# More PSUM banks for the scatter, slots and gather of a two-layer decoder step's expert loop, and the scatter's add ahead of the next low part

## The chip, the cores and the metric

The kernel runs on one NeuronCore of a Trainium2 chip. The metric is the device time of one execution in microseconds (us): the median of three runs.

## The reference

One inference step of a two-layer decoder trunk for 256 prompt tokens and 64 sample tokens, 320 in all, in float32. Each layer is a mixer (window attention, a short convolution, attention into a memory), a layer norm, a feed-forward part and another layer norm. The feed-forward part is a dense SwiGLU in layer 0; in layer 1, which takes half of the time, each token goes to two of eight SwiGLU experts:

```python
def _swiglu(x, wg, wu, wd):
    return (jax.nn.silu(x @ wg) * (x @ wu)) @ wd

def _moe(x, w_router, b_router, wg, wu, wd):
    ...
    top_v, top_i = lax.top_k(logits, TOP_K)          # 2 of 8
    top_w = jax.nn.softmax(top_v, axis=-1)
    gates = jnp.sum(jax.nn.one_hot(top_i, N_EXPERTS) * top_w[..., None], axis=1)
    for e in range(N_EXPERTS):
        y = y + gates[:, e:e + 1] * _swiglu(xt, wg[e], wu[e], wd[e])
```

The width is 1024, the hidden width 2816.

## The kernel before

**Precision.** A float32 product is made from three fast ones. Each weight is split into a high part (a rounded copy) and a low part (weight minus high part), each activation likewise, and TensorE (PE) adds high x high, low x high and high x low in PSUM.

**Units.** Weights stream from HBM in units of 1 MB (128 x 2048 numbers). SyncE (SP) issues the load of a unit into a ring of 11 buffers as soon as the unit that held the buffer is done. ScalarE (ACT) writes the high part into one of three buffers (`hi_moe`, L771), so it waits for the load and for the unit three back. VectorE (DVE) writes the low part over the raw weights (`lo_moe`, L1050) when the high part is there. Both work two units ahead of PE: in iteration m they make the parts of unit m+2, and ACT can begin when unit m-1 is done.

**The expert loop.** Every engine runs a hardware loop of its own over pairs of experts (`Fori`, `step`); with these inputs it has 4 steps. Experts take at most 128 tokens at a time, in 128 slots each. A pair is 66 units, 33 an expert (n = 0 to 32; j = 0 or 1 is the expert). The hidden width is cut into halves h = 0 to 5 of 512 (the last of 256). Gate units fill PSUM bank 2 + h % 2, up units bank 4 + h % 2, and the down units (first at n = 8) add into banks 0 and 1. A unit is twelve matmuls of 512 columns (L1910 to L1912 or L1894 to L1896), and its last matmul raises `unit_done`. ACT makes silu of the gate half (L1004), DVE multiplies it by the up half (L1423), PE turns the result into bank 6 (L1919, after the units in `TURN_AFTER`), and ACT and DVE split it (`hidden_hi`, `hidden_lo`, L1403).

**Around a pair's units.** Beside the units each step does this, all of it through PSUM bank 7 before the change:

- *Scatter* (j = 0, after units 0 to 5): PE multiplies the previous pair's outputs `ygh`, `ygl` by the slot matrices, four matmuls (L1864, L1865) for one of six parts g of 128 tokens by 512 columns; DVE adds the part to the sum (`add_back`, L1410).
- *Slots* (after units 6 and 7) and *gates* (after 8): PE transposes the one-hot matrices of this pair (L1849) and sums the gates (L1856); DVE copies (L1433) or reduces them.
- *Gather* (j = 1, after units 28 to 31): ten matmuls of 256 columns (L1841 to L1843) collect two of the eight blocks of the next pair's tokens; ACT and DVE split them (`gathered`, L966, and `tokens_lo`, L1370).

Since one bank serves them all, each of these waits on PE until DVE has emptied the bank of the one before it:

```python
pe.wait_ge(scat_cp, step * 6 + g)          # scatter g: add g-1 is done
pe.wait_ge(xe_lo, step * 4 + (c + 4))      # gather c: low part c-1 is done
```

Each engine works through its own list in order. In iteration n of the loop DVE had this order: multiply (n in `MULT_AT`), low part of unit m+2, hidden low part, then the add, copy or reduction that belongs to unit n-1.

**Tables.** ACT needs a function table for Silu. The program's table loads are put in when it is compiled; in the trace each step has one ahead of its first high part (L771) and one ahead of its first silu (L1004).

Of the kernel before, what the change touches and what calls it, by code (L numbers as in the profile page):

```python
# [23 lines left out]
F32 = mybir.dt.float32  # L24
# [4 lines left out]
ALU = mybir.AluOpType  # L29
ACT = mybir.ActivationFunctionType  # L30
# [9 lines left out]
T = NP + NS  # L40
# [17 lines left out]
AHEAD = HI_RING - 1  # L58
# [75 lines left out]
TURN_AFTER = {5: 0, 9: 1, 15: 2, 21: 3, 27: 4, 29: 5}  # L134
GATHER_AFTER = {28: 0, 29: 1, 30: 2, 31: 3}
SCATTER_AFTER = {n: n for n in range(6)}
SLOTS_AFTER = {6: 0, 7: 1}
GATES_AFTER = 8
ONE_HOT_AT = 14
for (_k, _h), _n in LAST_UNIT.items():  # L140
    assert all(n > _n for n, hs in (SILU_AT.items() if _k == "g" else [(n, x) for n, xs in MULT_AT.items() for x in xs]) if hs == _h)
# [78 lines left out]
def build_trunk(nc, A, O):  # L220
    with ExitStack() as ctx:
# [33 lines left out]
        ident = take("ident", [P, P])  # L255
# [499 lines left out]
        def _(act):  # L755
# [207 lines left out]
            def gathered(first, c, bank=7):  # L963

                act.wait_ge(gath_mm, first + (c + 1))
                act.activation(xeh[:, 2 * c:2 * c + 2, :], ps[:, bank, :].rearrange("p (f s) -> p f s", s=2 * P),  # L966
                               ACT.Copy).then_inc(xe_hi, 1)
# [24 lines left out]
                residual(k)  # L992
            for c in range(1, 4):
                gathered(0, c, FIRST_BANK[c])
            act.activation(row_f[:, 3:4], eps[:, 0:1], ACT.Copy).then_inc(e_silu, 1)
            act.wait_ge(rt_total, 1)
            total = act.value_load(total_i[0:1, 0:1], min_val=PAIRS, max_val=ROUNDS * PAIRS)
            with act.Fori(0, total) as step:
                for m in range(NPAIR):
                    j, n = divmod(m, NX)  # L1000
                    hi_moe(step, m + AHEAD)
                    if n in SILU_AT:
                        h = SILU_AT[n]
                        act.activation(sil[:, h % 2, 0:HIDDEN[h][1]], ps[:, 2 + h % 2, 0:HIDDEN[h][1]],  # L1004
                                       ACT.Silu).then_inc(e_silu, 1)
                    if n - 1 in TURN_AFTER:
                        hidden_hi(step * 12 + 6 * j, TURN_AFTER[n - 1])
                    if j == 1 and n - 1 in GATHER_AFTER:
                        gathered(step * 4 + 4, GATHER_AFTER[n - 1])
                    if n == NX - 1:  # L1010
                        act.wait_ge(unit_done, step * NPAIR + (N_DENSE + m + 1))
                        act.wait_ge(slot_cp, step * 3 + 3)
                        act.activation(ygh[:, j, :], ps[:, 0:2, :].rearrange("p b n -> p (b n)"), ACT.Copy,
                                       scale=gs[:, j:j + 1]).then_inc(y_hi, 1)
# [22 lines left out]
        def _(dve):  # L1037
# [8 lines left out]
            def lo_moe(step, m):  # L1046

                s = (m + MOE_FIRST) % RING_MOE
                dve.wait_ge(hi_done, step * NPAIR + (N_DENSE + m + 1))
                dve.tensor_tensor(low_moe[s][:, :], raw_moe[s][:, :],  # L1050
                                  high[(N_DENSE + m) % HI_RING][:, :].bitcast(F32), ALU.subtract).then_inc(lo_done, 1)
# [347 lines left out]
            def hidden_lo(at, h):  # L1399
                tiles = HIDDEN[h][1] // P  # L1400
                to = slice(HID_TILE[h], HID_TILE[h] + tiles)
                dve.wait_ge(e_hi, at + (h + 1))
                dve.tensor_tensor(hel[:, to, :], ps[:, 6, 0:P * tiles].rearrange("p (f s) -> p f s", s=P),  # L1403
                                  heh[:, to, :].bitcast(F32), ALU.subtract).then_inc(e_lo, 1)

            def add_back(first, g):

                half = slice(512 * (g % 2), 512 * (g % 2) + 512)
                dve.wait_ge(scat_mm, first + (g + 1))
                dve.tensor_tensor(acc[:, g // 2, half], acc[:, g // 2, half], ps[:, 7, :], ALU.add).then_inc(scat_cp, 1)  # L1410

            dve.wait_ge(acc_cp, 6)
            dve.wait_ge(rt_total, 1)
# [1 line left out]
            with dve.Fori(0, total) as step:  # L1415
                for m in range(NPAIR):
                    j, n = divmod(m, NX)
                    at = step * 12 + 6 * j
                    for h in MULT_AT.get(n, ()):
                        width = HIDDEN[h][1]  # L1420
                        dve.wait_ge(e_silu, at + (h + 2))
                        dve.wait_ge(unit_done, step * NPAIR + (N_DENSE + NX * j + LAST_UNIT["u", h] + 1))
                        dve.tensor_tensor(sil[:, h % 2, 0:width], sil[:, h % 2, 0:width], ps[:, 4 + h % 2, 0:width],  # L1423
                                          ALU.mult).then_inc(e_h, 1)
                    lo_moe(step, m + AHEAD)
                    if n - 1 in TURN_AFTER:
                        hidden_lo(at, TURN_AFTER[n - 1])
                    if j == 0 and n - 1 in SCATTER_AFTER:
                        add_back(step * 6, SCATTER_AFTER[n - 1])
                    if j == 0 and n - 1 in SLOTS_AFTER:  # L1430
                        i = SLOTS_AFTER[n - 1]
                        dve.wait_ge(slot_mm, step * 3 + (i + 1))
                        dve.tensor_copy(slot[:, i, 0:T], ps[:, 7, 0:T]).then_inc(slot_cp, 1)  # L1433
                    if j == 0 and n - 1 == GATES_AFTER:
                        dve.wait_ge(slot_mm, step * 3 + 3)
                        dve.tensor_reduce(gs[:, :], ps[:, 7, 0:4].rearrange("p (j c) -> p j c", c=2), AX, ALU.add
                                          ).then_inc(slot_cp, 1)
                    if j == 1 and n == ONE_HOT_AT:
                        one_hot(step + 1)
                        gate_columns(step + 1)  # L1440
                    if j == 1 and n - 1 in GATHER_AFTER:
                        tokens_lo(step * 4 + 4, GATHER_AFTER[n - 1])
                    if n == NX - 1:
                        dve.wait_ge(y_hi, step * 2 + (j + 1))
                        dve.scalar_tensor_tensor(ygl[:, j, :], ps[:, 0:2, :].rearrange("p b n -> p (b n)"), gs[:, j:j + 1],
                                                 ygh[:, j, :].bitcast(F32), ALU.mult, ALU.subtract).then_inc(y_lo, 1)
# [39 lines left out]
        def _(pe):  # L1486
# [359 lines left out]
            def slots_of(j):  # L1846

                for t, (t0, tn) in enumerate(TILES):
                    last = pe.transpose(ps[:, 7, t0:t0 + tn], onehot[0:tn, t, j, :].bitcast(F32), ident[0:tn, 0:tn])  # L1849
                last.then_inc(slot_mm, 1)  # L1850

            def gates_of():
# [23 lines left out]
            with pe.Fori(0, total) as step:  # L1876
                for m in range(NPAIR):
# [36 lines left out]
                    if n in TURN_AFTER:  # L1914
                        h = TURN_AFTER[n]
                        pe.wait_ge(e_h, at + (h + 2))
                        pe.wait_ge(e_lo, at + (h + 1))
                        for f in range(HIDDEN[h][1] // P):
                            last = pe.transpose(ps[:, 6, P * f:P * f + P], sil[:, h % 2, P * f:P * f + P], ident[:, :])  # L1919
                        last.then_inc(e_tr, 1)  # L1920
                    if j == 0 and n in SCATTER_AFTER:
                        g = SCATTER_AFTER[n]
                        if g == 0:
                            pe.wait_ge(y_lo, step * 2 + 1)
                            pe.wait_ge(xe_lo, step * 4 + 4)
                        else:
                            pe.wait_ge(scat_cp, step * 6 + g)
                        scatter(ps[:, 7, :], g, 0, True, False)
                        scatter(ps[:, 7, :], g, 1, False, True).then_inc(scat_mm, 1)
                    if j == 0 and n in SLOTS_AFTER:  # L1930
                        if SLOTS_AFTER[n] == 0:
                            pe.wait_ge(scat_cp, step * 6 + 6)
                        else:
                            pe.wait_ge(slot_cp, step * 3 + 1)
                        slots_of(SLOTS_AFTER[n])
                    if j == 0 and n == GATES_AFTER:
                        pe.wait_ge(slot_cp, step * 3 + 2)
                        pe.wait_ge(gc_done, step + 1)
                        gates_of()
                    if j == 1 and n in GATHER_AFTER:  # L1940
                        c = GATHER_AFTER[n]
                        if c == 0:
                            pe.wait_ge(slot_cp, step * 3 + 3)
                            pe.wait_ge(oh_done, step + 2)
                        else:
                            pe.wait_ge(xe_lo, step * 4 + (c + 4))
                        gather(c)

            pe.wait_ge(e_h, total * 12 + 1)
            pe.wait_ge(e_lo, total * 12 + 1)  # L1950
# [39 lines left out]
```

## Time and profile before

| | us |
|---|---|
| median of 3 runs | 1709.35 (1709.29 to 1710.72) |
| the profiled execution | 1703.73 |
| its span, first to last instruction | 1702.0 |
| expert loop in it, first unit to the last unit's end | 829.3 to 1683.0 |
| the first matmuls of steps 1 to 4 | 829.29, 1044.68, 1257.88, 1472.32 |

The profile is of one execution. Engine times are busy times; a matmul's end is modelled, and matmuls overlap, so the start-to-start distance of two matmuls is their real price, and the "idle before" of PE counts only from the modelled end of the matmul before. PEld is the weight load that precedes each matmul and runs beside the one before it.

### The profile page before, as it was taken

The page shows a single profiled execution, that of the slowest core. Times are in us where ns is not written, and L with a number is a line of the kernel's source. Part 1 is how long each engine was busy: PE and PEld are TensorE (multiplying, and loading weights), DVE is VectorE, ACT ScalarE, POOL GpSimd, SP SyncE. Part 2 cuts the span into 40 slices and gives each one's busy share as a digit, 9 for nine tenths or more (in the row PEclk, how much of TensorE's full clock was granted, in tenths as well). Part 3 has the DMA queues.
Part 4 walks back from the last instruction along what each step waited for, and adds up shares of the span by engine and source line. Part 5 has one row for each costly group of instructions (what it writes and reads, how often), then busy time and mean ns, then how long its engine had stood idle before and what let it go on. Part 6 is the DMA issues. An engine that isn't in the chain of part 4 may idle for free.

```text
span 1702.0 us, 23565 instructions
## 1 busy us (share of the span) xinstructions
PE 1615.1 (95%) x9231; PEld 1413.1 (83%) x9231; DVE 1134.3 (67%) x1048; ACT 934.7 (55%) x947; POOL 62.1 (4%) x114
## 2 busy tenths in 40 slices
PE   6999999999998999998899998999989999899996
PEld 6999898999997999897678886788867888678885
DVE  4545655644435445655678887788867888778887
ACT  3544443433323644443557776577755777657775
POOL 4112000000000020001000000000000000000000
PEclk8999999999999999999999999999999999999998
DMA  9745433344443443343589997899978999789991
GB/s 292 251 127 185 122 124 124 116 151 154 150 149 100 125 153 124 104 145 136 177 283 366 364 368 249 283 365 364 368 239 278 364 365 368 254 277 365 365 325 56
DMA packets 214085, 394.63 MB, mean 232 GB/s; under 512 B 8032, under 2 KB 98544, under 8 KB 213952
## 3 DMA queue, kind: packets, MB, share of 16 engines
q1 hardware_dynamic: 208576, 379.08, 64.9%
q0 software_dynamic: 5408, 14.06, 2.7%
q8 instruction: 81, 1.33, 0.3%
q14 instruction: 20, 0.16, 0.0%
HBM read 390.32 MB, written 4.76 MB: 232 GB/s over the span
## 4 chain that ended last, share of the span: by engine, by line
PE 87%; DVE 5%; issue 4%; ACT 3%; DMA 1%; SPq 0%; DVEq 0%; ACTq 0%
PE ps L1489 12%; PE ps L1491 12%; PE ps L1490 12%; PE ps L1910 9%; PE ps L1912 9%; PE ps L1911 9%; PE ps L1894 4%; PE ps L1896 4%; PE ps L1895 4%; ACT high L771 2%; PE ps L1919 1%; PE ps L1638 1%; PE ps L1744 1%; PE ps L1738 1%; PE ps L1612 1%
## 5 line engine op out<-in xcount | busy, mean ns | idle before, releaser
L1050 DVE TENSOR_TENSOR low<-raw,high 128x2048 fp32r<-128x2048 f32 x266 | 608.6, 2291 | 154.5 <-ACT high L771 154.5
L771 ACT ACTIVATE high<-raw 128x2048 fp32r<-128x2048 f32 x266 | 509.7, 1918 | 273.7 <-PE ps L1912 168.0
L1489 PE MATMUL ps<-xh,high 128*128 128x320 f32 x1088 | 341.8, 314 | 10.3 <-DVE xl L1229 9.4
L1059 DVE TENSOR_TENSOR low<-raw,high 128x2048 fp32r<-128x2048 f32 x90 | 205.9, 2291 | 214.4 <-ACT high L764 214.2
L1490 PE MATMUL ps<-xh,low 128*128 128x320 f32 x1088 | 337.8, 310 | 0.0
L1491 PE MATMUL ps<-xl,high 128*128 128x320 f32 x1088 | 337.7, 310 | 0.0
L1910 PE MATMUL ps<-high,xeh 128*128 128x512 f32 (+1 forms) x768 | 293.5, 382 | 8.1 <-issue 7.3
L1911 PE MATMUL ps<-low,xeh 128*128 128x512 f32 (+1 forms) x768 | 289.1, 376 | 0.0
L1912 PE MATMUL ps<-high,xel 128*128 128x512 f32 (+1 forms) x768 | 288.9, 376 | 0.0
L764 ACT ACTIVATE high<-raw 128x2048 fp32r<-128x2048 f32 x90 | 171.9, 1910 | 172.7 <-PE ps L1491 156.5
L1489 PEld LDWEIGHTS ps<-xh,high 128*128 128x128 f32 x1088 | 206.2, 190 | 19.8 <-issue 19.0
L1490 PEld LDWEIGHTS ps<-xh,low 128*128 128x128 f32 x1088 | 206.4, 190 | 0.0
L1491 PEld LDWEIGHTS ps<-xl,high 128*128 128x128 f32 x1088 | 206.2, 190 | 0.0
L1910 PEld LDWEIGHTS ps<-high,xeh 128*128 128x128 f32 x768 | 144.9, 189 | 38.3 <-issue 8.6
L1912 PEld LDWEIGHTS ps<-high,xel 128*128 128x128 f32 x768 | 145.1, 189 | 29.4
L1911 PEld LDWEIGHTS ps<-low,xeh 128*128 128x128 f32 x768 | 144.9, 189 | 26.8
L1894 PE MATMUL ps<-high,heh 128*128 128x512 f32 x352 | 140.8, 400 | 0.0
L1896 PE MATMUL ps<-high,hel 128*128 128x512 f32 x352 | 139.3, 396 | 0.0
L1895 PE MATMUL ps<-low,heh 128*128 128x512 f32 x352 | 138.9, 395 | 0.0
L1896 PEld LDWEIGHTS ps<-high,hel 128*128 128x128 f32 x352 | 66.0, 187 | 16.0
L1894 PEld LDWEIGHTS ps<-high,heh 128*128 128x128 f32 x352 | 66.1, 188 | 14.7
L1895 PEld LDWEIGHTS ps<-low,heh 128*128 128x128 f32 x352 | 66.2, 188 | 14.6
(323 smaller groups left out, 1731.4 us busy)
## 6 DMA issues: line engine op xcount, KB each, us to landing
raw<-in_exp_w_gate_dram SPq DMA_DIRECT2D x90, 1024.0 KB, 5.3
raw<-in_exp_w_up_dram SPq DMA_DIRECT2D x88, 1024.0 KB, 5.3
raw<-in_exp_w_down_dram SPq DMA_DIRECT2D x88, 1024.0 KB, 5.3
raw<-in_w_in_dram SPq DMA_DIRECT2D x37, 1024.0 KB, 5.4
raw<-in_ffn_w_gate_dram SPq DMA_DIRECT2D x11, 1024.0 KB, 5.3
raw<-in_ffn_w_up_dram SPq DMA_DIRECT2D x11, 1024.0 KB, 5.3
raw<-in_ffn_w_down_dram SPq DMA_DIRECT2D x11, 1024.0 KB, 5.0
raw<-in_w_o_dram SPq DMA_DIRECT2D x8, 1024.0 KB, 5.0
```

Source lines behind the costliest of these rows:

```text
L771: act.activation(high[(N_DENSE + m) % HI_RING][:, :], raw_moe[s][:, :], ACT.Copy).then_inc(hi_done, 1)
L1050: dve.tensor_tensor(low_moe[s][:, :], raw_moe[s][:, :], high[(N_DENSE + m) % HI_RING][:, :].bitcast(F32), ALU.subtract).then_inc(lo_done, 1)
L1059: dve.tensor_tensor(low[n % RING][:, :], raw[n % RING][:, :], high[n % HI_RING][:, :].bitcast(F32), ALU.subtract).then_inc(lo_done, 1)
L1489: pe.matmul(out, wh, ah, start=first, stop=False)
L1490: pe.matmul(out, wl, ah, start=False, stop=False)
L1491: return pe.matmul(out, wh, al, start=False, stop=last)
L1894: pe.matmul(out, heh[:, tile, :], wh[:, c], start=i == 0 and k == 0, stop=False)
L1895: pe.matmul(out, heh[:, tile, :], wl[:, c], start=False, stop=False)
L1896: last = pe.matmul(out, hel[:, tile, :], wh[:, c], start=False, stop=i == NBLK - 1 and k == 1)
L1910: pe.matmul(out, xeh[:, k, slots], wh[:, c], start=k == 0, stop=False)
L1911: pe.matmul(out, xeh[:, k, slots], wl[:, c], start=False, stop=False)
L1912: last = pe.matmul(out, xel[:, k, slots], wh[:, c], start=False, stop=k == KD - 1)
```

## The change

- Scatter part g goes to bank 7, 0, 1, 7, 0, 1; its wait is now for the add three parts back, and parts 0 to 2 wait for no add. Banks 0 and 1 are free of expert outputs from the pair's end until unit 8.
- The slot matrix of expert 0 goes to bank 7, that of expert 1 to bank 6, where the hidden halves are turned: it waits for the hidden low part of half 0, and the turn after unit 9 waits for its copy. The gates wait for the first slot copy only.
- Gather c goes to bank 7, 3, 4, 7: the two in the middle wait for the last silu and for a product of halves, the fourth for the low part of the first.
- On DVE the scatter's adds, the slot copies and the gate reduction move ahead of the low part of unit m+2. The gather's low parts stay behind it.
- ACT computes a one-element Silu at the head of each step, so the Silu table is loaded there.

```diff
+SCATTER_BANK = (7, 0, 1, 7, 0, 1)
+SLOT_BANK = (7, 6)
+GATHER_BANK = (7, 3, 4, 7)
...
-            act.activation(row_f[:, 3:4], eps[:, 0:1], ACT.Copy).then_inc(e_silu, 1)
+            act.activation(row_f[:, 2:3], eps[:, 0:1], ACT.Copy).then_inc(e_silu, 1)
...
             with act.Fori(0, total) as step:
+                act.activation(row_f[:, 3:4], eps[:, 0:1], ACT.Silu)
                 for m in range(NPAIR):
...
-                        gathered(step * 4 + 4, GATHER_AFTER[n - 1])
+                        gathered(step * 4 + 4, GATHER_AFTER[n - 1], GATHER_BANK[GATHER_AFTER[n - 1]])
...
-                dve.tensor_tensor(acc[:, g // 2, half], acc[:, g // 2, half], ps[:, 7, :], ALU.add).then_inc(scat_cp, 1)
+                dve.tensor_tensor(acc[:, g // 2, half], acc[:, g // 2, half], ps[:, SCATTER_BANK[g], :],
+                                  ALU.add).then_inc(scat_cp, 1)
...
-                    lo_moe(step, m + AHEAD)
-                    if n - 1 in TURN_AFTER:
-                        hidden_lo(at, TURN_AFTER[n - 1])
                     if j == 0 and n - 1 in SCATTER_AFTER:
                         add_back(step * 6, SCATTER_AFTER[n - 1])
                     if j == 0 and n - 1 in SLOTS_AFTER:
                         i = SLOTS_AFTER[n - 1]
                         dve.wait_ge(slot_mm, step * 3 + (i + 1))
-                        dve.tensor_copy(slot[:, i, 0:T], ps[:, 7, 0:T]).then_inc(slot_cp, 1)
+                        dve.tensor_copy(slot[:, i, 0:T], ps[:, SLOT_BANK[i], 0:T]).then_inc(slot_cp, 1)
                     if j == 0 and n - 1 == GATES_AFTER:
                         dve.wait_ge(slot_mm, step * 3 + 3)
...
+                    lo_moe(step, m + AHEAD)
+                    if n - 1 in TURN_AFTER:
+                        hidden_lo(at, TURN_AFTER[n - 1])
...
-                        tokens_lo(step * 4 + 4, GATHER_AFTER[n - 1])
+                        tokens_lo(step * 4 + 4, GATHER_AFTER[n - 1], GATHER_BANK[GATHER_AFTER[n - 1]])
...
+                        if j == 0 and h == 1:
+                            pe.wait_ge(slot_cp, step * 3 + 2)
                         for f in range(HIDDEN[h][1] // P):
...
-                        else:
-                            pe.wait_ge(scat_cp, step * 6 + g)
-                        scatter(ps[:, 7, :], g, 0, True, False)
-                        scatter(ps[:, 7, :], g, 1, False, True).then_inc(scat_mm, 1)
+                        elif g >= 3:
+                            pe.wait_ge(scat_cp, step * 6 + (g - 2))
+                        scatter(ps[:, SCATTER_BANK[g], :], g, 0, True, False)
+                        scatter(ps[:, SCATTER_BANK[g], :], g, 1, False, True).then_inc(scat_mm, 1)
...
                         else:
-                            pe.wait_ge(slot_cp, step * 3 + 1)
+                            pe.wait_ge(e_lo, at + 2)
                         slots_of(SLOTS_AFTER[n])
                     if j == 0 and n == GATES_AFTER:
-                        pe.wait_ge(slot_cp, step * 3 + 2)
+                        pe.wait_ge(slot_cp, step * 3 + 1)
                         pe.wait_ge(gc_done, step + 1)
                         gates_of()
...
+                        elif c == 1:
+                            pe.wait_ge(e_silu, at + 7)
+                        elif c == 2:
+                            pe.wait_ge(e_h, at + 6)
                         else:
-                            pe.wait_ge(xe_lo, step * 4 + (c + 4))
-                        gather(c)
+                            pe.wait_ge(xe_lo, step * 4 + 5)
+                        gather(c, GATHER_BANK[c])
```

## Rows read from the trace of the kernel before

**Rows 1.** The page's first part: busy time (share of the span) and instructions.
```profile
PE 1615.1 (95%) x9231; PEld 1413.1 (83%) x9231; DVE 1134.3 (67%) x1048; ACT 934.7 (55%) x947; POOL 62.1 (4%) x114
```

**Rows 2.** Windows: length, busy by engine, granted clock, DMA share, GB/s.
```profile
1044.60:1257.80 213.20, 204.53 (x960) 165.46 (x960) 174.51 (x111) 144.40 (x100) 0.00 (x0) 1.00 0.92 326
...
1044.60:1088.00 43.40, 38.63 (x166) 29.43 (x167) 29.35 (x23) 22.81 (x16) 0.00 (x0) 1.00 0.71 239
1088.00:1159.00 71.00, 71.00 (x338) 58.31 (x337) 60.88 (x35) 52.14 (x35) 0.00 (x0) 1.00 1.00 359
```

**Rows 3.** Waits in the expert loop: total us, times, longest us.
```profile
ACT high L771 <- PE ps L1912: 168.0, 171, 3.8
...
PE ps L1864 <- DVE acc L1410: 13.3, 12, 2.1
...
PE ps L1910 <- issue: 7.3, 3, 2.6
PE ps L1841 <- DVE xel L1370: 5.3, 8, 0.7
...
PE ps L1849 <- DVE slot L1433: 3.0, 4, 0.8
...
PE ps L1856 <- DVE slot L1433: 1.7, 4, 0.5
PE ps L1849 <- DVE acc L1410: 1.4, 4, 0.5
```

**Rows 4.** Timeline around unit 3's end, step 2: start, us, instruction, idle before.
```profile
1058.61 2.29 DVE L1050 TENSOR_TENSOR low<-raw,high 128x2048 fp32r<-128x2048 f32 x1 [2.33 <-ACT high L771]
...
1059.97 0.39 PE L1912 MATMUL ps<-high,xel 128*128 128x512 f32 x1
1060.39 1.91 ACT L771 ACTIVATE high<-raw 128x2048 fp32r<-128x2048 f32 x1 [1.81 <-PE ps L1912]
...
1060.82 0.68 DVE L1410 TENSOR_TENSOR acc<-acc,ps 128x512 f32<-128x512 f32 x1
1061.42 0.68 DVE L1423 TENSOR_TENSOR sil<-sil,ps 128x512 f32<-128x512 f32 x1
...
1061.56 0.50 PE L1864 MATMUL ps<-ygh,slot 128*128 128x512 f32 x1 [1.20 <-DVE acc L1410]
...
1061.90 0.39 PE L1865 MATMUL ps<-ygl,slot 128*128 128x512 f32 x1
...
1062.13 0.40 PE L1864 MATMUL ps<-ygh,slot 128*128 128x512 f32 x1
...
1062.34 2.29 DVE L1050 TENSOR_TENSOR low<-raw,high 128x2048 fp32r<-128x2048 f32 x1 [0.23 <-ACT high L771]
```

**Rows 5.** Timeline of PE ahead of the third gather of step 1.
```profile
1032.71 0.40 PE L1896 MATMUL ps<-high,hel 128*128 128x512 f32 x1
1033.18 0.39 PE L1841 MATMUL ps<-onehot,xtokh 128*128 128x256 f32 x1
```

**Rows 6.** Timeline of PE: step 1's second scatter and after; step 3's first matmul.
```profile
838.14 0.50 PE L1864 MATMUL ps<-ygh,slot 128*128 128x512 f32 x1 [2.12 <-DVE acc L1410]
...
839.53 0.63 PE L1911 MATMUL ps<-low,xeh 128*128 128x512 f32 x1
...
842.52 0.46 PE L1912 MATMUL ps<-high,xel 128*128 128x512 f32 x1
...
1257.88 0.50 PE L1910 MATMUL ps<-high,xeh 128*128 128x512 f32 x1 [2.59 <-issue]
```

**Rows 7.** Groups in the loop: count, busy us, mean ns, idle before.
```profile
L1004 ACT ACT_TABLE_LOAD x4 | 5.1, 1283 | 0.1
...
L1433 DVE CAST slot<-ps 128x320 fp32r<-128x320 f32 x8 | 3.9, 482 | 0.0
...
L995 ACT ACTIVATE row_f<-eps 128x1 f32<-128x1 f32 x1 | 0.2, 194 | 0.0
```

**Rows 8.** SP's weight loads in step 2: time from issue to landing.
```profile
DMA to landing us min/median/max: 4.8/5.3/6.6
```

More of the change, by code:

```diff
@@ L1848, in slots_of @@
                 for t, (t0, tn) in enumerate(TILES):
-                    last = pe.transpose(ps[:, 7, t0:t0 + tn], onehot[0:tn, t, j, :].bitcast(F32), ident[0:tn, 0:tn])
+                    last = pe.transpose(ps[:, SLOT_BANK[j], t0:t0 + tn], onehot[0:tn, t, j, :].bitcast(F32), ident[0:tn, 0:tn])
                 last.then_inc(slot_mm, 1)
```

## The prediction

> **What bounds the kernel now.** I read the page first: PE is busy 95% of the span [rows 1], but its busy time is made of overlapping matmuls, so I looked at stretches of the expert loop, the only part that the diff touches. Step 2 lasts 213.2 us. The 71 us from its unit 10 on (1088 to 1159) keep PE busy all the time at a granted clock of 1.00; the first ten units, with scatter, slots and gates, leave it idle for 43.40 - 38.63 = 4.8 us [rows 2]. Then the waits. ACT waits for PE, 168.0 us behind gate and up units alone, and no wait of ACT for a load is listed. PE waits for the DVE operations that empty bank 7: 13.3 us for adds, 5.3 for gathered low parts, 3.0 + 1.4 + 1.7 around slots and gates; besides, 7.3 us of "issue" in three waits [rows 3], at the three turns of the loop. So PE is the bound, with two kinds of holes: the waits on bank 7, and the turn of the loop, which the change leaves alone.
>
> **One stall, followed.** Rows 4 show the scatter behind unit 3. The unit's last matmul starts at 1059.97 and has ended when ACT begins the next high part at 1060.39. DVE has begun a low part at 1058.61 and reaches the add of the earlier scatter, done long since, only behind it, at 1060.82. PE's scatter waits for that add and starts at 1061.56 [rows 4]. The distance from the matmul before is 1.59 us where back-to-back matmuls take 0.23 (1061.90 to 1062.13), and the following one comes after 0.34. The loss is 1.36 + 0.11 = 1.47 us, against a listed idle of 1.20: I add 0.27 to each idle of this kind, or 0.16 where the short matmuls of another operation follow.
>
> **What the change removes.**
> - Scatter: 13.3 us idle in 12 waits [rows 3], with 12 x 0.27 = 3.2: 16.5 us. Part g now waits for the add three parts back.
> - Slots and gates: 3.0 + 1.4 + 1.7 = 6.1 us in 12 waits [rows 3], with 12 x 0.16 = 1.9: 8.0 us.
> - Gather: 5.3 us in 8 waits [rows 3]; 0.16 for the four behind a unit (0.6), nothing for the four behind transposes, whose usual handover is longer. The third gather shows no idle but a distance of 0.47 for 0.23 [rows 5]: 4 x 0.24 = 1.0. Together 6.9 us.
> - One of two table loads a step: 4 x 1.28 us of ACT [rows 7]. I count nothing: in this stretch ACT idles 1.81 us before a high part, waiting for PE [rows 4]. Without that cover it would be 5.1 us.
>
> Sum: 16.5 + 8.0 + 6.9 = 31.4 us.
>
> **What it adds, and whether a stall comes back elsewhere.** A unit is 12 matmuls, 12 x 0.23 = 2.8 us, a scatter four, 0.9 us (estimates from the spacing in rows 4). Call T the end of unit m-1; times follow from T.
> - *The add ahead of the low part.* The scatter ends at about T + 1.0, the add takes 0.68 [rows 4]: done at T + 1.7. The low part can't start before ACT's high part, 1.91 us from T + 0.02 [rows 4], is done at about T + 1.95. The add fits into a gap in which DVE idles today, with 0.25 us to spare. Where a multiply comes too (unit 3 to 4), it takes 0.68 [rows 4] from T, still before the scatter ends. After unit 5 four transposes come ahead of the scatter; at four matmuls' price for them at most, the add ends at T + 2.6 and the low part is 0.7 late. That doesn't reach PE: a low part takes 2.29 [rows 4], ends at T + 4.3 on time and is read at T + 0.9 + 2.8 + 0.9 + 2.8 = T + 7.4. The margin is 3.1 us, 2.8 + 2.8 - 4.3 = 1.3 where no scatter stands between.
> - *DVE's load.* Low part, add and, once, multiply: 2.29 + 0.68 + 0.68 = 3.65 us against PE's 3.7 a unit in the scatter; elsewhere a slot copy of 0.48 [rows 7] or a hidden low part (as wide as the add, so 0.68) in place of the add: 2.8 to 3.5, for units that with slots or gates take longer than 2.8. Behind unit 7 multiply and copy stand ahead of one low part, which may then be late by some tenths; the margin there is over 1.3. So no stall on the low parts.
> - *New waits on PE.* The second slot transposes wait for the hidden low part of half 0. It stands on DVE behind the low part that ends at T + 4.3 to 5.0 (T is unit 5's end), so it is done by T + 5.7; PE gets there two units, a scatter, transposes and the first slots later, after at least 0.9 + 2.8 + 2.8 = 6.5. Behind this wait are unit 8 and all later ones, so its lateness would count in full; it has 0.8 us at least. The turn after unit 9 waits for a copy made behind unit 7, the second and third gather for a silu and a product that are two units old, the fourth for a low part three units old. Nothing.
> - *The one-element Silu* at the head of a step: 0.19 us by the like Copy [rows 7], in ACT's way to the third unit's high part. That unit's margin is the 3.1 us above. Nothing; without the cover 4 x 0.2 = 0.8.
> - *DMA.* No load moves, and SP is released by `unit_done` as before. Faster units ask for more: 66 units of 1.05 MB in 213.2 - 31.4/4 = 205.4 us, 337 GB/s, where the stretch from 1088 to 1159 gets 359 now [rows 2].
>
> **The clock.** The second scatter of step 1 starts after 2.12 us of idle. The matmuls from 839.53 to 842.52 are then 0.427 us apart, seven distances: PE is at the lower of its two levels, 1.2 GHz, instead of 2.4 [rows 6]. That costs 7 x 0.2 = 1.4 us, and as the idle goes, I take this fall to go with it. The loop's turns leave idles of up to 2.59 us [rows 6], and the change does not touch these. A fall at a turn would cost about as much, 1.4, so three turns are worth 0 to 4.2 us. The Trainium skill (TensorE: Matmul & The Clock Gate, on the clock gate's warm-up) says that the gate is either at half or at full rate and that the same kernel switches at different points from run to run. By that rule the 1.4 us might not come back, and the sum would be 31.4 instead of 32.8; no row here can decide it, as I have one execution.
>
> **The sum.** 31.4 + 1.4 = 32.8 us. Against the profiled execution, 1703.73 us, that makes 1670.9. The three timed runs have a median of 1709.35, 5.6 us above it, which I carry over: 1676.5 us.
>
> **Rivals.**
> - *Part of the stalls comes back (14 in 100).* If only the scatter gains 16.5 us, because slots and gathers find another wait (the hidden low part, or DVE's order, in which the gather's low parts stay behind the weights'), the time is 1692.9. For it: 0.25 and 0.8 us are small margins. Against it: the large ones, 1.3 to 3.1 us, stand behind them.
> - *No change, since the weights set the pace (5 in 100).* DMA's share is 1.00 from 1088 to 1159 [rows 2]. If it could do no more over a step, PE would lose at loads what it gains at banks: 1709. Against it: no wait for a load, and a load lands after 4.8 to 6.6 us in all of step 2 [rows 8], with the scatter's DMA share of 0.71 inside [rows 2], so no queue builds up.
> - *Slower: the low parts held behind the adds (3 in 100).* DVE takes its list in order, so an add whose scatter is not done holds up the low part behind it, and PE stands for that two units later. It costs PE nothing until the add ends 3.1 us after the high part, at T + 5.0. To eat 31.4 us over the four steps' 24 adds it would have to be 1.3 us later each, T + 6.3; at T + 6.8 the time would be 1709.35 - 32.8 + 24 x 1.8 = 1720. The rows give T + 1.7. The Trainium skill (PSUM — Partial Sum Buffer, Engine vs sequencer instructions) states this rule: queues of ScalarE and VectorE are strictly first in, first out. The trace agrees, since in rows 4 a finished scatter's add stands 2.2 us behind a low part; the same rule makes the old order costly and the new one risky.
>
> **How the numbers follow.** The forecast, all stalls gone, has 78 in 100 and gives 1676.5; by itself 1671 (the profiled execution's 5.6 us as a gain) to 1682 (four falls of the clock at 1.4 us more than today). The range reaches towards the partial case until it leaves out 2 in 10: 1671 to 1686. Within 0.2% (3.4 us), about what a measurement of this kernel can tell from no change, lies the case of the loads, 5 in 100; slower 3; the rest, 92, is faster.
>
> **What would show it.** Right: PE's waits for L1410's add, the slot copies and the gathered low parts vanish from the list; units 0 to 9 of step 2 take some 6 us less than 43.4; the adds stand ahead of their low parts and DVE's waits for ACT's high part shrink there; the "issue" waits remain; one table load a step. Wrong: a new wait of PE for a low part or the hidden low part in units 2 to 10, or waits of ACT for loads, or more stretches at 1.2 GHz behind the loop's turns.

## The result, and the profile after

The changed kernel takes 1665.2 us (1663.78 to 1671.1, 4 runs) against 1709.32 in four runs of the kernel before: a ratio of 0.9752 (95% interval 0.9723 to 0.9781). It is faster, as forecast, but the forecast was 1676.5 us in 1671 to 1686, so the time lies below the range. The profiled execution of the changed kernel spans 1662.1 us, 39.9 less than that of before; the sum had promised 32.8.

What I had said would vanish did vanish. The list of waits in the loop (total, times, longest us):

```profile
ACT high L774 <- PE ps L1917: 148.9, 171, 1.8
DVE low L1054 <- ACT high L774: 107.6, 198, 2.0
...
DVE acc L1414 <- PE ps L1870: 6.2, 11, 0.8
PE ps L1915 <- DVE xel L1374: 5.1, 3, 1.8
```

Against [rows 3], no wait of PE for an add, a slot copy or the next gather is left, and it is DVE that now waits for a scatter; its waits for ACT's high part fall from 151.5 us in the kernel before to 107.6. But the 7.3 us of "issue" at the turns of the loop have shrunk too, to three waits of 5.1 us in all, which the view puts down to a gathered low part. Windows of the same stretches as in [rows 2] (length, busy by engine, granted clock, DMA share, GB/s):

```profile
1032.00:1068.60 36.60, 36.56 (x163) 29.40 (x164) 29.93 (x23) 21.70 (x16) 0.00 (x0) 1.00 0.85 280
1068.60:1139.60 71.00, 71.00 (x340) 58.66 (x338) 60.69 (x35) 52.70 (x35) 0.00 (x0) 1.00 1.00 360
```

Units 0 to 9 of step 2 keep PE busy for 36.56 of 36.60 us, where they left 4.8 us idle; the stretch behind them is as it was. The timeline around unit 3's end, as in [rows 4]:

```profile
1046.06 0.39 PE L1869 MATMUL ps<-ygh,slot 128*128 128x512 f32 x1
...
1046.69 0.68 DVE L1428 TENSOR_TENSOR sil<-sil,ps 128x512 f32<-128x512 f32 x1
...
1047.29 0.68 DVE L1414 TENSOR_TENSOR acc<-acc,ps 128x512 f32<-128x512 f32 x1
1048.20 2.29 DVE L1054 TENSOR_TENSOR low<-raw,high 128x2048 fp32r<-128x2048 f32 x1 [0.24 <-ACT high L774]
```

The scatter runs on at once; multiply and add fit in ahead of the low part, which still starts when ACT's high part is done, with 0.24 us to spare.

**Where the time came from.** From the start times of the same matmuls in both timelines, all four steps together (us):

| part of the loop | before | after | less | said |
|---|---|---|---|---|
| units 0 to 9, with scatter, slots, gates | 175.3 | 146.5 | 28.8 | 24.5 + 1.4 clock |
| units 10 up to the second expert's unit 28 | 585.3 | 585.2 | 0.1 | 0 |
| the last five units, with the gather | 84.2 | 75.4 | 8.7 | 6.9 |
| three turns of the loop | 8.5 | 6.3 | 2.2 | 0 |
| the last step's end to the final scatter | 0.5 | 1.4 | -0.9 | 0 |
| loop | 853.8 | 814.8 | 39.0 | 32.8 |

In the 28.8 us are two stretches of PE at 1.2 GHz that the changed kernel does not have: the one that I had counted in step 1 (1.4 us), and a second at the start of step 3, behind the 2.59 us of idle in [rows 6]. A window there, in the kernel before, has a granted clock of 0.50:

```profile
1259.10:1262.10 3.00, 3.00 (x8) 2.32 (x7) 2.29 (x1) 0.56 (x1) 0.00 (x0) 0.50 0.28 104
```

Step 3's units 0 to 9 took 44.39 us before, step 2's 42.84: 1.55 us.

### The profile page after: what moved, and what is told of

Same layout as the page of the kernel before. It is cut to its first block, busy times and chain, and to the rows that moved or that the text cites. A ratio compares the mean times of both kernels' runs of the same rounds, so it can differ in the third digit from the quotient of the medians.

```text
span 1662.1 us, 23553 instructions
## 1 busy us (share of the span) xinstructions
PE 1603.0 (96%) x9231; PEld 1413.8 (85%) x9231; DVE 1135.4 (68%) x1048; ACT 928.8 (56%) x947; POOL 62.3 (4%) x114
## 3 DMA queue, kind: packets, MB, share of 16 engines
HBM read 390.32 MB, written 4.76 MB: 238 GB/s over the span
## 4 chain that ended last, share of the span: by engine, by line
PE 93%; DVE 3%; ACT 2%; issue 1%; DMA 1%; SPq 0%; DVEq 0%; ACTq 0%
PE ps L1494 12%; PE ps L1495 12%; PE ps L1496 12%; PE ps L1915 10%; PE ps L1917 10%; PE ps L1916 10%; PE ps L1899 5%; PE ps L1901 5%; PE ps L1900 5%; PE ps L1926 1%; PE ps L1643 1%; PE ps L1749 1%; PE ps L1869 1%; PE ps L1743 1%; PE ps L1870 1%
## 5 line engine op out<-in xcount | busy, mean ns | idle before, releaser
L1917 PEld LDWEIGHTS ps<-high,xel 128*128 128x128 f32 x768 | 144.3, 188 | 28.8
```

Of the source, the lines that this page charges most:

```text
L1917: last = pe.matmul(out, xel[:, k, slots], wh[:, c], start=False, stop=k == KD - 1)
```

## The experiments

The table has, for each kernel, the loop's parts as above (sums in us), the median length of PE's taken loop branch, and in how many steps a stretch at 1.2 GHz lies in units 0 to 9 ("falls"; one profiled execution each).

| kernel | units 0-9 | gather | turns | end | branch | falls | loop |
|---|---|---|---|---|---|---|---|
| before | 175.3 | 84.2 | 8.5 | 0.5 | 5.57 | 2 | 853.8 |
| changed | 146.5 | 75.4 | 6.3 | 1.4 | 4.82 | 0 | 814.8 |
| e1 order alone | 151.4 | 84.1 | 8.7 | 0.6 | 5.75 | 3 | 829.8 |
| e2 banks alone | 152.8 | 75.4 | 6.0 | 1.4 | 4.76 | 0 | 820.9 |
| e3 gather alone | 173.9 | 75.4 | 6.1 | 1.4 | 4.86 | 1 | 842.1 |
| e4 Silu alone | 178.2 | 84.1 | 8.6 | 0.6 | 5.53 | 4 | 856.7 |
| e5 order, held loads | 147.6 | 84.1 | 2.9 | 0.6 | 3.72 | 0 | 820.3 |
| e6 changed, held loads | 146.6 | 75.4 | 1.9 | 1.4 | 3.46 | 0 | 810.5 |
| e7 changed, PE two pairs a turn | 146.4 | 75.4 | 2.6 | 1.4 | 4.91 | 0 | 811.0 |
| e8 changed, gather's low first | 147.9 | 75.4 | 6.2 | 0.2 | 4.81 | 1 | 815.0 |
| e9 changed, with e6, e7 and part of e8 | 146.6 | 75.4 | 1.0 | 0.2 | 3.38 | 0 | 808.5 |
| e10 changed, again | 146.4 | 75.4 | 6.0 | 1.4 | 4.76 | 0 | 814.4 |
| e11 before, held loads | 179.0 | 84.1 | 2.3 | 0.5 | 3.52 | 2 | 851.2 |

(Branch: median of the three taken ones; of the one that e7 and e9 have. The branch not taken at the loop's end lasts 0.08.)

**e1: the order on DVE alone.**
```diff
-                    lo_moe(step, m + AHEAD)
-                    if n - 1 in TURN_AFTER:
-                        hidden_lo(at, TURN_AFTER[n - 1])
                     if j == 0 and n - 1 in SCATTER_AFTER:
                         add_back(step * 6, SCATTER_AFTER[n - 1])
...
+                    lo_moe(step, m + AHEAD)
+                    if n - 1 in TURN_AFTER:
+                        hidden_lo(at, TURN_AFTER[n - 1])
```


> Kernel before with one part of the change: on VectorE the scatter's adds, the slot copies and the gate reduction stand ahead of the next low part; one bank for all, as before. Theory A (the order by itself frees bank 7 in time: the add ends 1.7 us after its unit, the next scatter comes 3.7 us after it): PE's waits on the adds and slot copies vanish, step 2 from its first matmul to unit 10 falls from 42.8 us to 36.6 to 37.5, the gather stays at 21.0 us, the turn of the loop at 2.7 to 3.0; about 26 us less in the loop, 1682 us. Theory B (it is the banks that free PE, one bank still makes PE wait for the add): over 1695 us with waits on L1410's add left.


Measured: 1680.3 us, ratio 0.9846 (0.9823 to 0.9869). Theory A. PE's waits in the loop:
```profile
PE ps L1910 <- issue: 7.5, 3, 2.6
PE ps L1841 <- DVE xel L1370: 5.2, 8, 0.7
```
The waits on adds and copies are gone with one bank for all of them, and step 1's units 0 to 9 take 36.77 us. The other three steps take 38.2, over the 36.6 to 37.5 expected, each with a stretch at 1.2 GHz behind a turn with 2.26 to 2.65 us of idle. The loop is 24.0 us shorter, where about 26 were expected.

**e2: the banks alone**, with the old order and without the Silu (its edit against the changed kernel):
```diff
 SCATTER_BANK = (7, 0, 1, 7, 0, 1)
 SLOT_BANK = (7, 6)
 GATHER_BANK = (7, 3, 4, 7)
...
+                    lo_moe(step, m + AHEAD)
                     if j == 0 and n - 1 in SCATTER_AFTER:
...
-                    lo_moe(step, m + AHEAD)
```


> Kernel before with the other part alone: scatter, slots and gather over several banks as in the changed kernel, VectorE's old order, two table loads a pair. Theory A (a bank is needed again only three scatters later, so a late add does no harm): no wait in the scatter; one is left ahead of the first slots, which need the last add: it stands behind a low part and the hidden low part and ends 1.2 us late, 5 us over four steps. Gather and turn as in the changed kernel. Some 5 us above the changed kernel, 1670 us. Theory B (the order is what counts): most of the scatter's 16.5 us stays, 1685 us or more.


Measured: 1673.48 us, ratio 0.981 (0.9783 to 0.9838). Theory A here too:
```profile
PE ps L1853 <- DVE acc L1413: 5.5, 4, 1.4
PE ps L1914 <- DVE xel L1373: 4.8, 3, 1.7
```
The loop is 6.1 us longer than the changed kernel's, where 5 were expected. One wait a step is left, 5.5 us in all, ahead of the first slots, where the last add stands behind the low part and the hidden low part. So either half of the change removes the scatter's stalls by itself. The halves differ at the first slots, which the order frees, and in the gather, which the banks free.

**e3: the gather's banks alone.**
```diff
+GATHER_BANK = (7, 3, 4, 7)
...
+                        elif c == 1:
+                            pe.wait_ge(e_silu, at + 7)
+                        elif c == 2:
+                            pe.wait_ge(e_h, at + 6)
                         else:
-                            pe.wait_ge(xe_lo, step * 4 + (c + 4))
-                        gather(c)
+                            pe.wait_ge(xe_lo, step * 4 + 5)
+                        gather(c, GATHER_BANK[c])
```


> Kernel before with the gather's banks alone (7, 3, 4, 7). Theory A (the stall ahead of the fourth gather is also what lengthens the loop's turn): the last five units with the gather fall from 21.0 to 18.9 us a step, the taken branch of PE from 5.5 to 4.8 us and the idle at the turn from 2.4-2.6 to 1.6-1.8: 8.7 + 2.2 us less, and 0.9 back at the loop's end, so 1699 us. Theory B (the turn shortened for a reason outside the gather): the branch stays at 5.5 us, about 1701.5 us.


Measured: 1695.06 us, ratio 0.9936 (0.9912 to 0.996). Theory A in the trace: gather 75.4, branch 4.86 us, idle of 1.50 to 1.70 us at the turns. The loop is 11.7 us shorter, where 8.7 + 2.2 - 0.9 = 10.0 were expected; 1.4 of the rest are the fall of the clock in step 3 that this profile does not have. The shorter turn comes with the gather's banks.

**e4: the Silu alone.**
```diff
...
             with act.Fori(0, total) as step:
+                act.activation(row_f[:, 3:4], eps[:, 0:1], ACT.Silu)
```


> Kernel before with the one-element Silu at the head of each step alone: one table load a step instead of two. Theory A (the load that goes is hidden by ScalarE's wait for PE): no change within 0.1%, PE's waits as before, the branch of PE at 5.5 us. Theory B (ScalarE's time at the step's head reaches PE): 4 x 1.1 = 4.3 us less, 1705 us, with a shorter turn.


Measured: 1708.63 us, ratio 1.0002 (0.9988 to 1.0017): theory A, the load that goes was hidden. Its profiled execution, at 1714.42 us the longest of ten, has a fall of the clock in units 0 to 9 of every step.

**The branch itself.** The profile has a row for the instruction that closes PE's loop (start at the end of the row). In the kernel before, in step 1:
```profile
L1876 PEldq COMPARE_BRANCH  x1: 5571/5571/5571, 1038.7 to 1038.7; - x1
```
in the changed kernel:
```profile
L1881 PEldq COMPARE_BRANCH  x1: 4799/4799/4799, 1026.9 to 1026.9; - x1
```
and in the kernel before the one of ACT, whose loop is short:
```profile
L998 ACTq COMPARE_BRANCH  x4: 40/45/45, 1042.4 to 1683.0; - x4
```
PE's sequencer takes the branch some 3.6 us ahead of the end of the engine's last matmul (at 1042.3 before, at 1030.5 after), with work queued for that long, and the engine stands still for the rest. The lead is the same in both; the branch is 0.8 us shorter. DMA traffic by queue in the half microsecond in which one 16 KB packet moves on the instruction queue, before (1041.5 to 1042.0):
```profile
q1 hardware_dynamic: 42, 0.11, 57.2%
q8 instruction: 1, 0.02, 12.5%
```
and after (1029.0 to 1029.5):
```profile
q1 hardware_dynamic: 54, 0.22, 107.3%
q8 instruction: 1, 0.02, 12.0%
```
The columns are packets, MB and time as a share of 16 engines. The packet comes 2.8 to 3.3 us behind the branch's start before and 2.1 to 2.6 after, amid weight packets (q1) both times. That made a theory: the fetch of the loop head's instructions waits behind weight loads. In the kernel before a load had been issued about 1.1 us ahead of the branch, in the changed one 0.3.

**e5 and e6: the loads that SP issues at the ends of units 30 and 31 held back to the end of unit 32**, so that none runs during the branch:
```diff
-                    sp.wait_ge(unit_done, step * NPAIR + (N_DENSE - RING_MOE + m + 1))
+                    held = {8: 2, 9: 1}.get(m, 0)
+                    sp.wait_ge(unit_done, step * NPAIR + (N_DENSE - RING_MOE + m + 1 + held))
```
On the order alone (e5):


> The order alone (as e1_order) with the two weight loads that SyncE issues in a step's last two units held back until the last unit is done, so that no weights move while PE takes its loop branch. Theory A (the fetch of the loop head's instructions queues behind weight packets, and the idle at the turn decides on the clock's fall): the taken branch falls from 5.6 us to below 4.8, the idle at the turn from 2.3-2.6 to below 1.8, the three stretches at 1.2 GHz behind the turns go; 3 x 0.8 + 3 x 1.5 = 7 us less than the order alone, 1673 us. Theory B (the branch's length has to do with the stall ahead of the fourth gather, not with transfers): branch 5.6 us, falls of the clock as before, 1680 us.


On the changed kernel (e6):


> The changed kernel with the same two loads held back. Theory A (fetch behind weight packets): branch below 4.8 us, by as much a shorter idle at three turns: 1 to 3 us less, 1663 us. Theory B: branch 4.8 us, 1665 us.


Measured: e5 1671.55 us, ratio 0.979 (0.9762 to 0.9818); e6 1663.23, ratio 0.9739 (0.9711 to 0.9767). Theory A in both. In e6, from 1027.5 to 1028.0, the instruction packet moves alone:
```profile
q8 instruction: 1, 0.02, 12.9%
```
It comes 0.6 to 1.1 us behind the branch's start:
```profile
L1882 PEldq COMPARE_BRANCH  x1: 3460/3460/3460, 1026.9 to 1026.9; - x1
```
Over all profiles, the packet starts 3.1 to 3.4 us behind the branch's start in nine branches (before, e1, e4), 2.3 to 2.6 in sixteen (changed, e2, e3, e7, e8, e10) and 0.9 to 1.6 in the ten with held loads. From the packet's start to the branch's end it is 2.3 to 2.7 us in all 35; it is the time up to the packet that differs. Without weight packets it is short. Why it is longer in the first group than in the second is less sure: the last load was issued 1.1 us ahead of the branch in each of the nine and 0.3 in each of the sixteen, but no run moves that distance by itself. In e5 the stall ahead of the fourth gather is still there, the idle at the turns is 0.35 to 0.77 us, and the three falls of the clock that e1 had are gone.

**e7: PE's loop over two pairs a turn** (`twos` is half of `total`).
```diff
...
-            with pe.Fori(0, total) as step:
-                for m in range(NPAIR):
+            with pe.Fori(0, twos) as two:
+                for mm in range(2 * NPAIR):
+                    step, m = two * 2 + mm // NPAIR, mm % NPAIR
```


> The changed kernel with PE's loop over two pairs a turn: one taken branch in place of three. Theory A (the idle between two steps is the branch's fetch and nothing else): at the two seams without a branch PE goes on within 0.4 us, 2 x 1.8 = 3.6 us less, 1661.5 us. Theory B (the idle is the wait for the gathered low part that the trace names as releaser): the seams stay at 2 us, 1665 us.


Measured: 1663.68 us, ratio 0.9728 (0.9707 to 0.9749). Theory A in the trace: at a seam without a branch the next step's first matmul follows in the usual 0.23 us:
```profile
1034.31 0.39 PE L1906 MATMUL ps<-high,hel 128*128 128x512 f32 x1
1034.54 0.40 PE L1920 MATMUL ps<-high,xeh 128*128 128x512 f32 x1
```
So the gathered low part, which the list of waits named, was not what PE waited for. The time is 1.5 us below the changed kernel's first median, in different rounds, which is too little to call; the loop's 3.8 us in the trace are clear.

**e8: the gather's low parts ahead of the weights' on DVE too.**
```diff
+                    if j == 1 and n - 1 in GATHER_AFTER:
+                        tokens_lo(step * 4 + 4, GATHER_AFTER[n - 1], GATHER_BANK[GATHER_AFTER[n - 1]])
                     lo_moe(step, m + AHEAD)
...
-                    if j == 1 and n - 1 in GATHER_AFTER:
-                        tokens_lo(step * 4 + 4, GATHER_AFTER[n - 1], GATHER_BANK[GATHER_AFTER[n - 1]])
```


> The changed kernel with the gathered low parts ahead of the weights' low parts on VectorE too. Theory A (the turn is the branch): the turns stay at 2.0 us, only the 0.9 us that the last step's end had lost comes back; within 1 us of the changed kernel unless the later weight low parts reach PE. Theory B (the wait for the gathered low part): the three turns and the end shrink by over 1 us each, 1661 us.


Measured: 1670.77 us, ratio 0.9777 (0.9757 to 0.9797). Theory A in the trace: the turns stay (6.2 us), though the list of waits now puts them down to a weights' low part, and the end falls from 1.4 to 0.2. The time is not within 1 us of the changed kernel's. One fall of the clock follows a turn with 1.82 us of idle. The loop is no shorter than the changed kernel's, and the 5 us that the medians differ lie mostly ahead of it: the loop begins at 834.6 us in this profile and at 828.3 in the changed kernel's, with the same code up to there.

**e9: the changed kernel with the held loads, PE's loop over two pairs and the last gathered low part ahead; e10: the changed kernel again, e11: the held loads in the kernel before**, on one chip. The edit of e9 beside those of e6 and e7:
```diff
+                    if j == 1 and n == NX - 1:
+                        tokens_lo(step * 4 + 4, 3, GATHER_BANK[3])
                     lo_moe(step, m + AHEAD)
...
-                    if j == 1 and n - 1 in GATHER_AFTER:
+                    if j == 1 and n - 1 in GATHER_AFTER and n < NX - 1:
```


> The changed kernel with three things more: the two loads held back at a step's end, PE's loop over two pairs a turn, and the last gathered low part ahead of the weights' low part. Theory A (the idle between steps is the instruction fetch, and what is left at the end is the gathered low part): seams of 0.2 to 0.8 us in place of 2.1, the end's 1.4 us down to 0.3, no stretch at 1.2 GHz in the loop; loop 809.0 us, about 6 us less than the changed kernel. Theory B (holding the loads back costs as much elsewhere once the turn is short): 1664 us.

> The changed kernel once more, unedited, against the kernel before on the same chip. Theory A (39 us in the loop by the traces, the rest of the first measured difference of 44 being differences between executions ahead of the loop): a difference of 40 to 42 us. Theory B (the kernel before regularly loses more at the turns, by more falls of the clock than its profile shows): 43 to 46 us.

> The kernel before with nothing changed but the two loads held back. Theory A (the turn is a matter of the instruction fetch alone, stalls or not): branch 3.6 us, idle at the turns below 1 us, no fall of the clock behind them; 3 x 1.9 us and two falls, about 8 us less than before. Theory B: the stall ahead of the fourth gather keeps the branch at 5 us or more, 3 us less at most.


Measured: e9 1659.11 us, ratio 0.972 (0.9692 to 0.9749); e10 1667.72 us, ratio 0.9758 (0.9731 to 0.9785), 40.8 us below the kernel before (1708.54); e11 1703.0 us, ratio 0.9977 (0.9957 to 0.9997).

e9 is theory A, with no stretch at 1.2 GHz in the loop, 8.6 us below the changed kernel in the same rounds and the fastest of all. e10 is theory A: 39 us lie in the loop, and the first comparison's 44.1 held some 3 us of differences between executions. e11 is neither theory in full. The branch is 3.52 us and the turns shrink by 6.2 us, as A says, but the loop gains 2.6 us and not 8:
```profile
PE ps L1865 <- DVE acc L1411: 17.4, 12, 2.7
```
The adds' stalls are now 17.4 us, not 13.3 [rows 3]. PE gets earlier to the second scatter of a step, but the add that it waits for stands behind ACT's work at the step's head and does not come earlier: that stall lasts 2.43, 2.68 and 2.28 us in steps 2 to 4, where it lasted 1.24, 1.10 and 1.22 before, and in step 3 the clock falls behind it. With these stalls in place, the idle at the turn had been covering part of them.

## Why the prediction came out wrong

**Right: the stalls, and that none comes back.** Each wait on bank 7 went, no low part reached PE late, and the new waits cost nothing. The margin of 0.25 us for the add is in the trace as 0.24. One table load a step is left, and the one that went was worth nothing (e4). The rival by which only part is gained, the rival of the loads and the slower one by the queue's order did not come: the adds do stand ahead of their low parts, and the scatter is done in time.

**Right in kind, too small: two terms.** Scatter, slots and gates gave 28.8 - 1.4 - 1.55 = 25.9 us for 24.5. The gather gave 8.7 us for 6.9. I had added nothing for the four waits behind transposes, taking the handover behind a transpose to be longer anyway, and that was wrong:

```profile
1028.85 0.39 PE L1841 MATMUL ps<-onehot,xtokh 128*128 128x256 f32 x1 [0.71 <-DVE xel L1370]
1018.22 0.36 PE L1846 MATMUL ps<-onehot,xtokh 128*128 128x256 f32 x1
```

The first row, of the kernel before, stands 0.98 us behind the start of the last transpose, the second, of the changed kernel, 0.03. Such a wait cost 0.95 us for a listed 0.71: 1.0 us in four. The other 0.9 us are the matmuls behind a wait, which start further apart: in the kernel before the third gather's first two start at 1033.18 and 1033.40, in the changed kernel at 1022.30 and 1022.42, and so it is in the fourth gather. e3 has the 8.7 us by itself.

**Wrong: "the turn of the loop, which the change leaves alone".** This is the step that failed, with its counterpart under DMA, that no load moves. I took the 2.4 to 2.6 us of "issue" as a fixed price. They are what is left of a branch that takes 3.3 to 5.8 us, by how the fetch of its target's instructions meets the weight loads. The change takes away the stall ahead of the fourth gather; after that the branch starts 0.3 us behind a load's issue, not 1.1, and its packet comes earlier: 2.2 us over three turns. e3 shows that the gather's banks bring it; e5 and e11, where the stall stays, that without the loads the branch is short all the same; e7 that without the branch there is no idle. That the 2.2 us come from the load's distance to the branch is argued from these.

The Trainium skill (Runtime: NRT & Kernel Launch, Instruction fetch mechanics) says that a taken branch to a target outside the instructions at hand forces a fetch by DMA before execution goes on. The trace agrees: there is one 16 KB packet inside each of PE's taken branches, which last 4.8 to 5.7 us in the two kernels, while the branch of ACT's short loop takes 0.045 us.

**Wrong by omission: the clock behind the turns.** I expected one fall of the clock to go, and it went. I allowed for more falls behind the turns but not for fewer. Over all profiles of kernels whose turns last as in the kernel before (before, e1, e4), 7 of 9 turns, with idles of 2.26 to 2.65 us, were followed by a stretch at 1.2 GHz; in those with the shorter turn (changed, e2, e3, e7, e8, e10), 1 of 16, with idles of 1.44 to 1.82. The length alone does not decide: the two without a fall had 2.33 and 2.36 us. Nor is 7 of 9 a rate, as six of the seven are from e1 and e4, whose profiled executions were each the longest of that kernel. That the shorter idle is what spares the clock fits e5, where only the loads were moved and e1's three falls went; each cost 1.3 to 1.6 us. The one profile of before shows one such fall. The Trainium skill (TensorE: Matmul & The Clock Gate, on the clock gate's warm-up) says that a kernel switches at different points from run to run. The runs agree in so far as the mean granted clock of the kernel before lies between 0.980 and 0.988 in the fifteen executions beside e9. I used this rule only on the one side.

**Not foreseen, a loss: the end.** The final scatter waits for the last gathered low part, which stands behind a weights' low part on DVE. Before, PE lost 0.3 us there (0.53 from matmul to matmul instead of 0.23); now it loses 1.2 (1.41). e8 and e9 take it back.

**The range.** Its lower end was the forecast less 5.6 us, the distance between the profiled execution and the median, and held nothing for the turns. The 6.2 us by which the loop beat the sum were enough to leave it, by 0.7 us. They are the turns' 2.2, the second fall's 1.55, 1.4 of scatter, slots and gates and 1.8 of the gather, less 0.9 at the end, and 0.1. The forecast missed the median by some 11 us, and the rest of that is not shown to be the change's work: 1.0 us lies outside the loop, and 4.2 are the 5.6 us that I carried over and that did not carry. The changed kernel's median is 1.4 us above its profile, and e10's equals it. So the size of the miss is in part chance, as e10's 40.8 us against the first 44.1 show too.

## What to carry to other kernels

Before calling an idle stretch at a loop's turn fixed, look for the branch in the trace: where the loop's code must be fetched, the turn depends on what else moves on the DMA engines then, and a change of timing elsewhere moves it. Holding two loads back made it 1.4 us shorter a turn than the changed kernel's. A stall on a shared buffer can be cured by more buffers or by emptying it sooner; here either did for the scatter, and it is worth testing each alone to see which waits only one of them frees. And a cure for one wait can be hidden behind another: the shorter turn gained 4 us in the changed kernel's loop (e6), but only 2.6 in the old one (e11), where the stalls took the rest.

## What the runs showed of the hardware

PE's taken loop branch lasts 3.3 to 3.9 us with the two loads held back (e5, e6, e9, e11), and 4.7 to 5.0 or 5.5 to 5.8 when its one 16 KB instruction packet comes amid weight packets. Idles of 2.26 to 2.65 us at the loop's turns were followed by a stretch at 1.2 GHz at 7 of 9 places, waits of 2.1 to 2.7 us for the second scatter's add at 5 of 7 (before, e3, e4, e11). The same code ahead of the loop took 827.8 to 837.0 us in the thirteen profiles; the two slowest (e4, e8) show a mean granted clock of 0.97 to 0.99 in the windows from 0 to 400 and from 400 to 800 us, the three fastest (changed, e6, e11) 0.99 in both; what makes it fall there was not studied.
